# One layer of a hybrid decoder: the last two levels of a triangular inversion in 32x32 blocks, and SyncE's short transfers in another order

## The reference

```
h = rms_norm(x, norm_mix)
p = h @ w_in
y_a, wkv_new, row_new = rwkv7_mix(p[..., :SHIFT_COLS], ...)      # 8 heads x 64
y_b, buf_new = conv_mix(p[..., SHIFT_COLS:], ...)
x = x + jnp.concatenate([y_a, y_b], axis=-1) @ w_out
h2 = rms_norm(x, norm_ffn)
x = x + moe_ffn(h2, ...)                                         # top 4 of 32 experts
...
def step(s, inp):                                                # the scan inside rwkv7_mix
    r_t, w_t, k_t, v_t, kk_t, b_t = inp
    sa = jnp.einsum('bhvk,bhk->bhv', s, kk_t)
    s = s * w_t[:, :, None, :] - sa[..., None] * b_t[:, :, None, :] + v_t[..., None] * k_t[:, :, None, :]
    y = jnp.einsum('bhvk,bhk->bhv', s, r_t)
    return s, y
...
def expert_block(args):
    gt = jnp.minimum(xe @ w_gate[e] + b_gate[e], SWIGLU_LIMIT)
    up = jnp.clip(xe @ w_up[e] + b_up[e], -SWIGLU_LIMIT, SWIGLU_LIMIT)
    return ((up + 1.0) * gt * jax.nn.sigmoid(SWIGLU_ALPHA * gt)) @ w_down[e] + b_down[e]
```

## Time and profile before

| | |
|---|---|
| median of 3 runs | 1164.1 us |
| lowest and highest | 1163.79, 1164.47 us |
| profiled execution, its own time | 1165.45 us |
| its span, first to last instruction | 1163.6 us |
| TensorE busy | 1122.2 us (96%) |
| VectorE, ScalarE, GpSimd busy | 529.1, 212.3, 34.1 us |
| read and written by DMA | 430.00 MB, mean 370 GB/s |
| TensorE's granted clock, mean | 0.999 |

### The profile page before, as it was taken

One profiled execution on the slowest core, in us unless ns is written; L12 is line 12 of the kernel. 1 busy time (PEld: TensorE's weight loads), 2 busy tenths in 40 slices (PEclk: granted clock), 3 DMA queues, 4 the chain that ended last, 5 costly groups with the idle time before them and its releaser, 6 DMA issues.

```text
span 1163.6 us, 16613 instructions
## 1 busy us (share of the span) xinstructions
PE 1122.2 (96%) x6608; PEld 480.4 (41%) x6608; DVE 529.1 (45%) x1123; ACT 212.3 (18%) x433; POOL 34.1 (3%) x47
## 2 busy tenths in 40 slices
PE   9999999999999999999999999999999999999997
PEld 7666786643333333333333333333333333333332
DVE  6999965337333333333333333333333333333333
ACT  3265642221111111111111111111111111110012
POOL 0002412000000000000000000000000000000000
PEclk9999999999999999999999999999999999999999
DMA  9724006999999999999999999999999999999995
GB/s 247 214 86 179 20 16 175 429 392 415 417 427 427 429 428 430 427 429 427 430 429 427 430 427 430 428 429 427 430 427 429 430 426 430 429 429 427 429 421 204
DMA packets 58587, 430.00 MB, mean 370 GB/s; under 512 B 16670, under 2 KB 29390, under 8 KB 34220
## 3 DMA queue, kind: packets, MB, share of 16 engines
q1 hardware_dynamic: 58288, 428.84, 89.7%
q10 hardware_dynamic: 260, 0.61, 0.2%
HBM read 424.92 MB, written 4.48 MB: 369 GB/s over the span
## 4 chain that ended last, share of the span: by engine, by line
PE 53%; DMA 29%; DVE 4%; issue 1%; ACT 1%; DVEq 0%; ACTq 0%
PE bank L2166 35%; DMA ring<-in_w_up_dram 26%; PE bank L2133 5%; DMA arena<-in_w_up_dram 3%; PE bank L2140 2%; PE bank L2086 2%; PE bank L1734 2%; DVE arena L2536 1%; DVE arena L2560 1%; PE bank L1312 1%; PE bank L1271 1%; PE bank L2174 1%; PE bank L2192 1%; PE bank L1320 0%; PE bank L278 0%
## 5 line engine op out<-in xcount | busy, mean ns | idle before, releaser
L2166 PE MATMUL bank<-arena 128*64 128x512 f32 x1540 | 344.2, 594 | 11.4 <-DMA arena<-in_w_up_dram 11.2
L2166 PE MATMUL bank<-ring,arena 128*64 128x512 f32 x1532 | 342.2, 594 | 11.8 <-DMA ring<-in_w_up_dram 11.0
L2166 PEld LDWEIGHTS bank<-arena 128*64 128x64 f32 x1540 | 108.0, 136 | 225.8 <-issue 197.9
L2166 PEld LDWEIGHTS bank<-ring,arena 128*64 128x64 f32 x1532 | 108.0, 137 | 225.2 <-issue 198.0
L2560 DVE TENSOR_TENSOR arena<-arena,bank 128x512 f32<-128x512 f32 x180 | 110.0, 680 | 0.0
L2549 DVE SCALAR_TENSOR_TENSOR arena<-bank,arena 128x512 f32<-128x512 f32 x31 | 23.3, 751 | 182.0 <-ACT arena L1928 182.0
L2536 DVE TENSOR_SCALAR arena<-bank 128x512 f32<-128x512 f32 x31 | 21.4, 692 | 179.9 <-PE bank L2174 179.9
L610 PE MATMUL bank<-arena,ring 128*128 128x336 f32 x352 | 102.5, 447 | 0.3 <-DVE arena L751 0.3
L2133 PE MATMUL bank<-arena 128*64 128x512 f32 x372 | 86.7, 599 | 4.3 <-DVE arena L2560 0.6
L1904 ACT COPY arena<-bank 128x512 f32<-128x512 f32 x31 | 18.2, 587 | 354.3 <-PE bank L2133 354.3
L610 PEld LDWEIGHTS bank<-arena,ring 128*128 128x128 f32 x352 | 65.8, 189 | 34.2 <-issue 2.9
(11 more groups left out here) (387 smaller groups left out, 785.5 us busy)
## 6 DMA issues: line engine op xcount, KB each, us to landing
ring<-in_w_gate_dram SPq DMA_DIRECT2D x32, 2048.0 KB, 29.8
arena<-in_w_up_dram SPq DMA_DIRECT2D x32, 2048.0 KB, 32.8
arena<-in_w_gate_dram SPq DMA_DIRECT2D x32, 2048.0 KB, 29.9
arena<-in_w_down_dram SPq DMA_DIRECT2D x31, 2048.0 KB, 35.4
ring<-in_w_down_dram SPq DMA_DIRECT2D x31, 2048.0 KB, 35.4
ring<-in_w_up_dram SPq DMA_DIRECT2D x29, 2048.0 KB, 32.9
ring<-in_w_in_dram SPq DMA_DIRECT2D x11, 1024.0 KB, 8.4
ring<-in_w_up_dram SPq DMA_DIRECT2D x11, 512.0 KB, 7.3
```

The source lines that it names most:

```text
L2166: mm = M.matmul(bank[64 * hb:64 * hb + 64, b, :], tokens(cc), rows[:, 512 * hb:512 * hb + 512], start=(cc == 0), stop=(w3 == 2 and cc == K ...
```

## The change

It has two parts.

*The inversion.* Level 4 multiplies only the 32x32 blocks on the diagonal, each on its own 32 rows and 32 columns of the array: `level4_g` 32 products of 32 moving columns for a half; `level4_a` 16 products of 32 columns for the transposed blocks, of which only the upper one is needed (`AT4`), and 32 of 64 columns for `A`, already crossed. VectorE masks 256 columns (`first_level`). Level 5 makes only the block that is missing: `level5_x` is 16 products of the off-diagonal block of `Nm` with `AT4`, VectorE negates them (`second_level`), `level5_y` is 16 products with the lower block of `A`, and ScalarE and VectorE copy 32 rows each, 256 columns, into `A` (`first_rows`, `second_rows`). `level5_x` waits for both copies of the right sides (`wc_ready`, `wc5_ready`), since it writes bank 0 and 1. ScalarE spreads the transposed 16x16 blocks in four instructions in place of eight. The samples' product moves ahead of the last step and to bank 5. Two small constants are added (`clow32`, `half2`).

*The queue.* The small loads of the norms and the router go ahead of the bias pieces, the kept rows ahead of the state stores, the prompt's state store and the final norm behind the fifth weight unit; GpSimd splits the biases once ScalarE has spread the blocks (`at0_ready` 2). Some tiles change place for it (`wr`, `brow`, `gffn2`, `ycg`).

```diff
-        E = [pair_tile(at_word(o, 512)) for o in (4736, 23424)]
+        E4 = [at_word(o, 8, 32) for o in (4736, 23424)]
+        E5 = [at_word(o, 8, 32) for o in (4992, 23680)]
...
-        G_BANK, AT_BANK = (7, 6), (4, 5)
-        A_BANK = {4: (2, 3), 5: (4, 2)}
+        G_BANK, A_BANK, X_BANK, Y_BANK = (7, 6), (4, 2), (0, 6), (4, 6)
...
+            for u in range(2):
+                sp.dma_start(gffn.rearrange("p (q h) -> p h q", q=4)[:, u], ...
             sp.wait_ge(out_stored, 16 * stores[0])
+            sp.wait_ge(S["atcol_ready"], 1)
+            sp.dma_start(wr, a["w_router"][0].rearrange("(c p) e -> p c e", c=KC)).then_inc(F["wr_in"], 16)
+            sp.dma_start(brow, a["b_router"].broadcast_to([P, NE])).then_inc(F["wr_in"], 16)
+            sp.dma_start(gffn2, a["norm_ffn"][0].rearrange("(c p) -> p c", c=KC),
...
+            sp.wait_ge(S["y5_done"], 1)
+            sp.dma_start(flat(xTk), xt_dram).then_inc(F["x_in"], 16)
             for j in range(NPAIR):
                 sp.wait_ge(S["sout_ready"], j + 1)
...
+            for p in range(2):
+                act.wait_ge(S["at_done"], p + 1)
+                nc.scalar.copy(AT4[p], tiles(G_BANK[p], 256)).then_inc(S["at_ready"], 1)
+                act.wait_ge(S["a_done"], p + 1)
+                nc.scalar.copy(tile_pairs(A[p].rearrange("p q j c -> p (q j) c")), tile_banks(A_BANK[p], C))\
+                    .then_inc(S["a_ready"], 1)
...
+            for p in range(2):
+                act.wait_ge(S["a_done"], 3 + p)
+                nc.scalar.copy(A[p][0:32].rearrange("p q j c -> p (q j) c")[:, :, 32:64], tiles(Y_BANK[p])[0:32])\
+                    .then_inc(S["first_rows"], 1)
...
+            def level4_g(p):
...
+                for u in range(8):
+                    for i in range(2):
+                        for b in range(2):
+                            g = rows32(i, b)
+                            mm = M.matmul(tiles(G_BANK[p])[g, u, :], Nm[p][g, u // 4, u % 4, 32 * b:32 * b + 32],
+                                          AT0[g, 8 * p + u, :], start=True, stop=True)
+                mm.then_inc(S["g_done"], 1)
...
+            def level5_x(p):
+                pe.wait_ge(S["at_ready"], p + 1)
+                if p == 0:
+                    pe.wait_ge(S["wc_ready"], 1)
+                    pe.wait_ge(S["wc5_ready"], 1)
...
-            level_g(4, 0)
-            level_g(4, 1)
-            level_a(4, 0)
-            level_a(4, 1)
-            level_g(5, 0)
-            level_g(5, 1)
-            level_a(5, 0)
-            level_a(5, 1)
-            pe.wait_ge(S["wc5_ready"], 1)
+            level4_g(0)
+            level4_g(1)
+            level4_a(0)
+            level4_a(1)
+            level5_x(0)
+            level5_x(1)
             pe.wait_ge(S["a0_ready"], 3)
-            pe.wait_ge(S["a_ready"], 2)
-            each(6, lambda i, j: A[2][side(i), 1, j, :], lambda i, j: Wc5[side(i), j, :],
+            pe.wait_ge(S["a_ready"], 1)
+            each(5, lambda i, j: A[2][side(i), 1, j, :], lambda i, j: Wc5[side(i), j, :],
                  64, C, True, True).then_inc(S["u5_done"], 1)
+            level5_y(0)
+            level5_y(1)
...
+            def second_rows(p):
+                dve.wait_ge(S["a_done"], 3 + p)
...
                 scan_sp(sp)
-                sp.wait_ge(S["y5_done"], 1)
-                sp.dma_start(flat(xTk), xt_dram).then_inc(F["x_in"], 16)
-                sp.wait_ge(S["w_done"], 5)
...
                 for k in range(NSLOT):
+                    if k == 5:
+                        sp.wait_ge(F["zp_copied"], 1)
+                        sp.dma_start(a["wkv_prompt"][0, 0].rearrange("(j h) v k -> (h v) j k", h=2), zpT)\
+                            .then_inc(out_stored, 16)
...
                 scan_pool(pool)
                 T = nc.gpsimd
-                pool.wait_ge(S["e_ready"], 4)
+                pool.wait_ge(S["at0_ready"], 2)
```

More of the change, by code:

```diff
@@ L153, in build @@
         sel2 = take(2, 32)
+        clow32, half2 = take(32), take(2)
+        assert cursor[0] <= mixer_start + 16832
         cursor[0] = mixer_start + 16832
@@ L1285, in level_g, with rows32 @@
[L1285 to L1306 removed]
+            def rows32(i, b):
+                return slice(64 * i + 32 * b, 64 * i + 32 * b + 32)
@@ new lines, in level4_a @@
+            def level4_a(p):
+                pe.wait_ge(S["e_ready"], p + 1)
+                pe.wait_ge(S["a0_ready"], p + 1)
+                for u in range(8):
+                    for i in range(2):
+                        g = rows32(i, 0)
+                        mm = M.matmul(tiles(G_BANK[p], 256)[g, u, :], A[p][g, u // 4, u % 4, 0:32], E4[p][g, u, :],
+                                      start=True, stop=True)
+                mm.then_inc(S["at_done"], 1)
+                pe.wait_ge(S["old_read"], 3 + p)
+                for u in range(8):
+                    for i in range(2):
+                        for b in range(2):
+                            g, at = rows32(i, b), C * (u // 2)
+                            mm = M.matmul(bank[rows32(i ^ (u % 2), b), A_BANK[p] + u % 2, at:at + C], E4[p][g, u, :],
+                                          A[p][g, u // 4, u % 4, :], start=True, stop=True)
+                mm.then_inc(S["a_done"], 1)
@@ new lines, in level5_x @@
+            def level5_x(p):
[3 more added lines that the diff above has]
+                    pe.wait_ge(S["wc5_ready"], 1)
+                for u in range(8):
+                    for i in range(2):
+                        g, at = rows32(i, 0), 32 * (u // 2)
+                        mm = M.matmul(bank[rows32(i ^ (u % 2), 1), X_BANK[p] + u % 2, at:at + 32],
+                                      Nm[p][g, u // 4, u % 4, 32:64], AT4[p][g, u, :], start=True, stop=True)
+                mm.then_inc(S["g_done"], 1)
@@ L1308, in each, with level5_y @@
+            def level5_y(p):
+                pe.wait_ge(S["e_ready"], 3 + p)
+                pe.wait_ge(S["a_ready"], p + 1)
+                for u in range(8):
+                    for i in range(2):
+                        g = rows32(i, 1)
+                        mm = M.matmul(tiles(Y_BANK[p])[rows32(i, 0), u, :], E5[p][g, u, :],
+                                      A[p][g, u // 4, u % 4, 32:64], start=True, stop=True)
+                mm.then_inc(S["a_done"], 1)
             def each(b, lhs, rhs, n_out, n_free, first, last, o=0):
@@ L1561, in scan_dve @@
             spread_a(0)
-            level(4, 0)
+            first_level(0)
             spread_a(1)
-            level(4, 1)
+            first_level(1)
             spread_a(2)
@@ L1570, in scan_dve @@
             z_affine(0)
-            level(5, 0)
-            level(5, 1)
+            second_level(0)
+            second_level(1)
             def negated(p, q, b):
```

131 lines of the change are left out of this document (46 added, 85 removed).

## The result

| | before | after |
|---|---|---|
| median of 5 runs | 1164.1 us | 1170.61 us |
| lowest and highest | 1163.28, 1164.57 | 1168.77, 1170.75 |
| ratio, 95% interval | | 1.0052 (1.0042 to 1.0063) |
| span of the profiled execution | 1163.6 us | 1168.8 us |
| TensorE's granted clock, mean | 0.999 | 0.992 |

The changed kernel is 6.5 us slower. The forecast was 1160.4, with 1159.4 to 1163.4 as its range, and 8% for slower. The two spans differ by 5.2 us only: the profiled execution of before took 1165.45 us, 1.35 above its median, that of after 1170.68, which is the median.

The account below looks back on a forecast made before the run. The end was taken to hang on the weight stream, positioned by TensorE at 290.57 us. Inversion 3.85 less 0.15 gives a 3.7 us gain, reordering 0: 1163.6 - 3.7 = 1159.9, from the median 1160.4; range 1159.4 to 1163.4.

Parts of the forecast that it names:

- What sets the end: Weight stream's position, set by TensorE at 290.57 us; shortening TensorE's way before the first expert moves the end as much.
- The products' time: Inversion's 32x32 products: 10 ns per instruction on four or eight tiles, 15.5 on two.
- The 25 ns: Overhead per matmul, some 60 cycles at 2.4 GHz; 448 would take 11.2 us, time 1166.3. Not followed.
- The order of the steps: Inversion from 152.35: products, masks, spreads and copies in turn bring chunk 0's product to 158.7 instead of 162.54, 3.85 us.
- 448 instructions: Inversion's levels after the change: 224 products, each two instructions in the trace, in place of 160 products.
- The queue half "worth 0": SyncE's reordering: first weight unit near 183, 13.6 us earlier, seventh still waiting for TensorE near 221.7; gain 0.
- GpSimd beside VectorE: GpSimd's five bias steps start near 153 and share SBUF with two VectorE spreads; 0.3 us added.
- The fourth: Rival: instructions on 32-row tiles keep 30 ns, chunk 0's product at 167.1, 4.5 us later, time 1168.6; chance 8%.

Follow-up runs that it names:

- runs 1 to 10: Ten follow-up kernels; not named singly: 4, kernel after plus five wide products, 1170.22 us; 6, kernel after with kept rows and router's small loads moved back, 1167.94 us.
- run 5: Kernel after with the first 32 products of the levels issued twice; 1170.68 us, a single run.
- run 8: Inversion alone changed, old SyncE order, with three and two wide products (128x512) added ahead of level 4's new A; 1167.21 us, ratio 1.0028.
- run 2: Kernel before with only SyncE's and GpSimd's new order, inversion as before; 1166.28 us, ratio 1.0027.
- run 9: Inversion alone changed, with products for every second head pair left out (112 instead of 224), copies and masks kept; 1159.32 us, ratio 0.9959.
- run 3: Kernel after with the kept rows' load back behind the state stores; 1168.05 us, ratio 1.0028.
- run 7: The hybrid: kernel before, old SyncE order, level 4's G and new A 64x64, its transposed block and level 5 in 32x32, 160 products; 1165.69 us, ratio 1.0011.
- run 1: Kernel before with the new inversion alone, SyncE's order and GpSimd's start as before; 1167.62 us, ratio 1.0029.
- the fills: Five wide 128x512 products without result, put in where TensorE stood still: on the kernel after 1170.22 us, on the inversion alone 1167.21 us.
- run 10: Kernel before with SyncE's new order alone, old inversion, kept rows' load back behind the state stores; 1164.08 us, ratio 0.9998.

## Why the prediction was wrong, point by point

- **What sets the end.** Right in the main. The end hangs on TensorE's position at the seventh unit: in the kernels above the seventh unit moved by +6.9, +3.8, +0.3, +2.8, +6.8, +6.8, +5.1, +1.7, +2.1, -4.1 and -0.6 us (after, runs 1 to 10) and the time by +6.5, +3.3, +1.9, +3.7, +5.9, +6.1, +3.4, +1.2, +2.9, -5.0 and -0.3. They agree within 1.7 us; the one is of a single execution, the other a median (of run 5 a single time). The spans follow less well: +5.2 after. The first DMA wait behind 600 us ends at 674.2 (640.13 + 34.10) against 669.0, also 5.2, though the unit of 290.57 went out 6.85 later. What lies between is not explained; the profiled execution of before was itself 1.35 us above its median, and where it lost that isn't known. In run 8 it is 2.3 us (last wait's end 1133.9 against 1134.0, seventh unit +2.1), in run 2 nothing (1134.3, +0.3).
- **The products' time.** Right, even cautious: 9.1 ns on four tiles, where I took 10. The 25 ns that I had estimated from the Trainium skill (TensorEngine Tiling (Array Packing), Instruction Overhead) are not seen between products on different tiles here.
- **The order of the steps.** Right as far as it can be seen: run 9, with half of the products.
- **That TensorE always has its instructions.** This is the step that failed. I counted the levels' work as "448 instructions" by their time and never asked how fast instructions arrive. There are 896 with the weight loads, and from the end of one gap to the end of the next, 127 or 128 pairs on, it is 3.38 (run 3), 3.49 and 3.56 (run 5), 3.66 (after), 3.83 (run 7) or 3.94 us (run 1): 27 to 31 ns for a pair. Without a stop, run 9 passed 127 pairs in 3.0 us, 23 ns each. The rate of the earlier trace rows, 30.1 ns for each record of the squares, lies in that bound, which is why no stop in the trace of before shows it. Cost: chunk 0's product at 164.69 instead of 158.7, 6.0 us, of which the clock at 0.50 behind 157.5 is a part that I can't divide off: with the fills and full clock it was 164.44 to 164.54. Not all 6.0 need be the instructions': run 9's 157.81 and at most 2 us for its missing half give 159.8 at the latest, an estimate, so 4.9 us are theirs at least.
- **TensorE's clock.** Not considered at all. The first fall cost 1.2 us behind chunk 0's product (run 8 against 1). In the kernel after TensorE had been idle for 2.25 us before it fell, in run 1 for 1.32 us and then for 0.48 of its second gap; with wide products in the gaps and one gap of 0.81 us (run 8) it didn't fall.
- **The queue half "worth 0".** Wrong in sign. Alone it cost 1.9 us in the median, by the kept rows' place (run 10), and beside the new inversion 3.8 us: from chunk 0's product to the seventh unit it is 67.6 us after and 228.25 - 164.43 = 63.8 in run 3. I had weighed the queue's order by SyncE's issue times and forgot that more than data goes through the DMA engines. The sizes were off too: bias pieces 10.59 us instead of 8.94, stores 17.68 instead of 11.24, so that the first unit left at 193.86, not 183. That cost nothing, as forecast, since the seventh waits for TensorE.
- **GpSimd beside VectorE.** I added 0.3 us. A spread of line 1580 took 1.27 us beside GpSimd's split and the next 0.76, against 0.68 in the earlier trace rows: 0.67 more together. A product of GpSimd's a little later took 1.41 us instead of 1.09. All that lay beside the wait for instructions and cost nothing visible. VectorE after:

```profile
153.39 1.27 DVE L1580 TENSOR_TENSOR arena<-arena 128x512 f32<-128x512 f32 x1
...
154.91 0.76 DVE L1580 TENSOR_TENSOR arena<-arena 128x512 f32<-128x512 f32 x1
```

- **The rivals.** The fourth, "slower: more tiles bring nothing", named 1168.6 and came nearest, with a wrong reason. Its 30 ns for a record are not the array's (9.1 ns) but the arrival of the instructions, and they hold on average over the levels: 164.69 - 152.25 = 12.4 us for 448 + 16 records, 27 ns each. With the third gap and the clock on top it becomes the measured loss.

The loss of 6.9 us at the seventh unit, divided by run 3 (chunk 0's product to the seventh unit: 62.9 before, 63.8 there, 67.6 after): 2.15 at chunk 0's product, 0.9 behind it, which I put down to the first fall of the clock (runs 1 and 8 give 1.2 for it), 3.8 by the kept rows' place, that is the third gap and the second fall.

## What to carry to other kernels

Where products become short, count instructions as well as nanoseconds: divide the time that the new order leaves for a stretch by its instructions (weight loads included, and every pass of a float32 product) and compare with the fastest rate that the trace holds over more than 256 of them. Splitting a product into blocks that skip zeros pays only while that rate isn't reached. "Issue" gaps at equal distances in the count of instructions, each shortly behind a packet of the instruction queue, are the sign, and large transfers put beside such a stretch can hold such a packet up.

## What the hardware showed that I had not expected

- TensorE stops for 0.26 to 2.9 us at places 127 or 128 load and product pairs apart, 1.2 to 1.6 us behind the landing of an instruction packet. From the end of one such stop to the end of the next it takes 3.38 to 3.94 us, in an order with 464 short records as in one with 160 products. No stop came where TensorE needed 3.8 us for a page, and once none where it needed 3.0 (run 9).
- A page of instructions is late where other transfers fill the DMA engines: with a share of 100% in 173.3 to 177.3 us TensorE's stop came in chunk 3, and none with 42%; with the old inversion the packet started at 176.8 behind the kept rows and at 174.5 without them (runs 2 and 10).
- Stops of this kind are enough to bring the granted clock to 0.50: for 10.2 us after 2.25 us of stop, for 3.4 us after 2.29 in chunk 3 and after 1.57 in the hybrid, for 13.7 us in run 5. It didn't fall behind 0.81 us (run 8) and 1.06 (run 5, in chunk 3).
- Records of 32 rows and 32 columns on four tiles of the array follow each other in 9.1 ns, as long as there are instructions.
